# A third Strassen step per chunk couple, with the sums of raw weights on GpSimd

## The reference

```python
u = rms_norm(h, norm_mlp_g)
h = h + square(relu(u @ mlp_w1)) @ mlp_w2          # 2048 -> 8192 -> 2048
gate = sigmoid(rms_norm(h, ple_norm_g) @ ple_w_gate)
h = h + gate * (p @ ple_w_proj)
```

## Time and profile before

| | value |
|---|---|
| median of 3 runs | 1187.95 us |
| the profiled execution | 1187.82 us |
| its span, first to last instruction | 1186.1 us |
| PE busy | 1179.5 us, 5426 matmuls |
| DVE busy | 813.8 us |
| ACT busy | 631.5 us |
| POOL busy | 22.6 us, 31 instructions |
| granted TensorE clock | 1.000 |

### The profile page before, as it was taken

How to read it: one execution, slowest core, us unless ns; L and a number is a source line. 1 busy time by engine, 2 the same in 40 slices (tenths; PEclk the granted TensorE clock), 3 DMA queues, 4 the chain that set the end, 5 groups by cost and what they waited for, 6 DMA issues and landing times.

```text
span 1186.1 us, 14260 instructions
## 1 busy us (share of the span) xinstructions
PE 1179.5 (99%) x5426; PEld 979.4 (83%) x5426; DVE 813.8 (69%) x1123; ACT 631.5 (53%) x876; POOL 22.6 (2%) x31
## 2 busy tenths in 40 slices
PE   9999999999999999999999999999999999999998
PEld 7888888888888888888888888888888888888886
DVE  5568867888776567755688755679655788676554
ACT  6745455666655554643455633456533466455443
POOL 1000100000000000000000000000000000000000
PEclk9999999999999999999999999999999999999999
DMA  9867673334358666865477865477865476886661
GB/s 344 320 177 242 215 236 137 107 111 136 107 163 282 205 216 203 283 222 194 143 249 246 278 214 191 168 240 236 287 195 195 161 249 243 275 262 204 216 205 49
DMA packets 110980, 249.26 MB, mean 210 GB/s; under 512 B 9664, under 2 KB 55744, under 8 KB 110912
## 3 DMA queue, kind: packets, MB, share of 16 engines
q1 hardware_dynamic: 110768, 248.34, 63.4%
q10 hardware_dynamic: 144, 0.01, 0.0%
HBM read 233.63 MB, written 14.68 MB: 209 GB/s over the span
## 4 chain that ended last, share of the span: by engine, by line
PE 99%; DMA 0%; DVE 0%; SPq 0%; ACT 0%; issue 0%
PE acc L1777 59%; PE acc L1803 11%; PE sc L1777 7%; PE tr L1803 7%; PE sc L1803 7%; PE sc L2003 1%; PE sc L1968 1%; PE tr L1920 1%; PE tr L1909 0%; PE sc L1909 0%; PE tr L2055 0%; PE tr L2056 0%; DMA w_raw<-in_nsa_w_in_units_dram 0%; PE acc L1892 0%; PE tr L2032 0%; PE tr L2038 0%
## 5 line engine op out<-in xcount | busy, mean ns | idle before, releaser
L1167 DVE TENSOR_TENSOR w_split<-w_raw,w_split 128x1024 fp32r<-128x1024 f32 x296 | 358.8, 1220 | 211.0 <-ACT w_split L726 210.3
L726 ACT ACTIVATE w_split<-w_raw 128x1024 fp32r<-128x1024 f32 x296 | 309.8, 1057 | 255.7 <-PE acc L1777 195.4
L1777 PE MATMUL acc<-w_split,b_split 128*128 128x512 f32 x1536 | 355.3, 390 | 0.0
L1777 PEld LDWEIGHTS acc<-w_split,b_split 128*128 128x128 f32 x1536 | 287.2, 188 | 59.2
L1777 PE MATMUL acc<-w_split,a_hi 128*128 128x512 f32 x1020 | 318.2, 393 | 0.9 <-DVE w_split L1163 0.8
L1777 PEld LDWEIGHTS acc<-w_split,a_hi 128*128 128x128 f32 x1020 | 188.5, 188 | 40.4 <-issue 1.6
L1777 PE MATMUL acc<-w_split,a_lo 128*128 128x512 f32 x510 | 198.9, 390 | 0.0
L737 ACT ACTIVATE w_split<-w_raw 128x1024 fp32r<-128x1024 f32 x98 | 101.1, 1054 | 64.7 <-PE acc L1777 22.7
L1181 DVE TENSOR_TENSOR w_split<-w_raw,w_split 128x1024 fp32r<-128x1024 f32 x84 | 100.9, 1218 | 50.3 <-ACT w_split L737 50.3
L1777 PEld LDWEIGHTS acc<-w_split,a_lo 128*128 128x128 f32 x510 | 95.7, 188 | 20.4
L1803 PE MATMUL acc<-w_split,a_hi 128*128 128x512 f32 x316 | 97.3, 389 | 0.0
(11 more groups left out here) (253 smaller groups left out, 1061.6 us busy)
## 6 DMA issues: line engine op xcount, KB each, us to landing
w_raw<-in_mlp_w_units_dram SPq DMA_DIRECT2D x256, 512.0 KB, 4.4
w_raw<-in_nsa_w_in_units_dram SPq DMA_DIRECT2D x76, 512.0 KB, 4.7
w_raw<-in_nsa_w_out_units_dram SPq DMA_DIRECT2D x32, 512.0 KB, 4.4
w_raw<-in_ple_w_gate_units_dram SPq DMA_DIRECT2D x32, 512.0 KB, 4.2
turn_dram<-s SPq DMA_DIRECT2D x52, 128.0 KB, 3.4
turn_dram<-junk SPq DMA_DIRECT2D x44, 128.0 KB, 3.7
v_slc<-turn_dram SPq DMA_DIRECT2D x22, 256.0 KB, 3.8
v_win<-turn_dram SPq DMA_DIRECT2D x22, 256.0 KB, 4.6
```

What stands on the lines that cost most here:

```text
L726: nc.scalar.activation(w_hi[:, u % SPLIT], w_raw[:, u % RAW], ACT.Copy).then_inc(hi_done, 1)
L1167: nc.vector.tensor_tensor(w_lo[:, u % SPLIT], w_raw[:, u % RAW], f32(w_hi[:, u % SPLIT]), ALU.subtract).then_inc(lo_done, 1)
L1777: last = nc.tensor.matmul(banks_of(c)[t][:], xs[:, kt, toks], ws[:, u % SPLIT, m * NW:(m + 1) * NW], start=(kt == 0 and n == 0), stop=(kt ...
```

## The change

`QUADS` becomes (2, 4, 6): three of eight feature steps use Strassen's products, in all seven couples. The four sums of each step move from DVE's program to POOL's, in one loop over all 21 steps; POOL waits for `direct`, each sum waits for the one before, ACT waits for `sums` as it did. DVE goes on to `t_lo`, waiting for `sums_hi`. The hooks move by a unit or so, since a unit that opens a step has no hook. `a_full`, `r_raw` and `r_split` grow to three steps, and a few small tensors change places so that `t_split`, `r_split` and `mixed` still fit over the attention's tensors.

```diff
-QUADS = (4, 6)
+QUADS = (2, 4, 6)
...
+def quads(c):
+    return QUADS
...
-QUAD_UNITS = [FIRST[c] + 2 * k for c in PAIR_NO for k in QUADS]
+QUAD_UNITS = [FIRST[c] + 2 * k for c in PAIR_NO for k in quads(c)]
+QUADS_TO = {c: sum(len(quads(b)) for b in PAIR_NO if b <= c) for c in PAIR_NO}
...
 (sync, up_pair)
-                        hidden_turns(n, s, 12)
+                        hidden_turns(n, s, 13)
...
 (sync, down)
-                    if s == 0 and q:
+                    if s == 1 and q:
                         turn_back(n + 1)
...
 (gpsimd, between power(8) and power(9))
+            for at, u in enumerate(QUAD_UNITS):
+                b11, b21 = (w_raw[:, u % RAW, m * NW:(m + 1) * NW] for m in range(2))
+                b12, b22 = (w_raw[:, (u + 1) % RAW, m * NW:(m + 1) * NW] for m in range(2))
+                pool.wait_ge(direct, at + 1)
+                nc.gpsimd.tensor_tensor(b11, b11, b12, ALU.add).then_inc(first_sums, 1)
+                pool.wait_ge(first_sums, 2 * at + 1)
+                nc.gpsimd.tensor_tensor(b12, b12, b22, ALU.add).then_inc(first_sums, 1)
+                pool.wait_ge(first_sums, 2 * at + 2)
+                nc.gpsimd.tensor_tensor(b22, b11, b22, ALU.add).then_inc(sums, 1)
+                pool.wait_ge(sums, 2 * at + 1)
+                nc.gpsimd.tensor_tensor(b21, b22, b21, ALU.add).then_inc(sums, 1)
...
 (scalar, up_pair)
-                        if s in (3, 5):
-                            hidden_out(c - 2, s // 2 - 1)
-                        if s in (13, 14):
-                            turned_hidden(s - 13, q)
+                        if s in (3, 6):
+                            hidden_out(c - 2, s // 3 - 1)
+                        if s == 14:
+                            turned_hidden(0, q)
...
 (scalar, down_pair)
+                    if s == 0 and q:
+                        turned_hidden(1, q)
...
 (vector, split_lo_pair)
-                    b11, b21 = (w_raw[:, (u - 1) % RAW, m * NW:(m + 1) * NW] for m in range(2))
-                    b12, b22 = (w_raw[:, u % RAW, m * NW:(m + 1) * NW] for m in range(2))
-                    dve.wait_ge(direct, at + 1)
-                    nc.vector.tensor_tensor(b11, b11, b12, ALU.add).then_inc(first_sums, 1)
-                    dve.wait_ge(first_sums, 2 * at + 1)
-                    nc.vector.tensor_tensor(b12, b12, b22, ALU.add).then_inc(first_sums, 1)
-                    dve.wait_ge(first_sums, 2 * at + 2)
-                    nc.vector.tensor_tensor(b22, b11, b22, ALU.add).then_inc(sums, 1)
-                    dve.wait_ge(sums, 2 * at + 1)
-                    nc.vector.tensor_tensor(b21, b22, b21, ALU.add).then_inc(sums, 1)
                     for half, v in enumerate((u, u - 1)):
                         dve.wait_ge(sums_hi, 2 * at + half + 1)
                         nc.vector.tensor_tensor(t_lo[:, half], w_raw[:, v % RAW], f32(t_hi[:, half]),
                                                 ALU.subtract).then_inc(lo_done, 1)
                     yield s
...
 (vector, up_pair: mix(c) now stands behind the other hooks of s = 15)
-                        if s == 4:
+                        if s == 5:
                             turn_hidden(n + 1)
-                        if s == 14:
+                        if s == 15:
                             turned_hidden(1, 0)
...
-                        if s in (4, 6):
+                        if s in (5, 7):
                             turn_hidden(n + s // 2 - 2)
-                        if s == 14:
+                        if s == 15:
                             turned_hidden(0, q)
...
 (vector, down_pair)
-                    if s == 0 and q:
+                    if s == 1 and q:
                         turned_hidden(1, q)
...
 (tensor, up_pair)
-                    if k not in QUADS:
+                    if k not in quads(c):
                         for half in range(2):
                             plain_unit(FIRST[c] + 2 * k + half, k, half, banks)
                         continue
-                    if k == QUADS[0]:
+                    if k == quads(c)[0]:
```

More of the change, by code:

```diff
@@ L153 @@
 HALVED = 4
-REST = (4 * UW + 8 * N_QUADS * P + 4 * NW
-        - (4 * HPG * SEQ + 128 + 2 * NW + 2 * NW + 2 * SEQ + NW + TT * HPG * N_CMP + 2 * DK + SEQ))
+REST = 494
 X_ROWS = 7
@@ L234, in trunk_layer @@
         causal = sb("causal", [P, SEQ])
+        hid = sb("hid", [P, HID])
+        cmp_neg = sb("cmp_neg", [P, TT, N_CMP])
+        cmp_one = sb("cmp_one", [P, TT, N_CMP])
+        gates = sb("gates", [P, TT, GATES])
+        fold = sb("fold", [2 * HID + 1, HID])
         rest = sb("rest", [P, REST])
+        with nc.sbuf_tensor("p_raw", [P, 2, SEQ], F32) as p_raw, \
+                nc.sbuf_tensor("pt_hi", [P, 2, SEQ], F32R) as pt_hi, nc.sbuf_tensor("pt_lo", [P, 2, SEQ], F32R) as pt_lo:
+            pass
+        p_t = sb("p_t", [P, 2, NW + SEQ])
         v_slc = sb("v_slc", [P, TT, NW])
@@ L243, in trunk_layer @@
         s1 = sb("s1", [P, 2, 2, SEQ])
[L244 to L247, removed]
         kc_rows, kc_sq = junk_act[0:N_CMP], junk[0:N_CMP, 0:NW]
@@ L254, in trunk_layer @@
         cmp_c = sb("cmp_c", [P, TT * HPG])
-        gates = sb("gates", [P, TT, GATES])
         hid_e, hid_rows = s0[0:HID, 1, 0], s0[0:HID, 1, 1]
-        hid = sb("hid", [P, HID])
         hid_pair = p_t[:].rearrange("p b s -> p (b s)")[:, 2 * NW:].rearrange("p (g h c n) -> p g h c n", g=G, h=2, c=4)
         ident = sb("ident", [P, P])
-        cmp_neg = sb("cmp_neg", [P, TT, N_CMP])
-        cmp_one = sb("cmp_one", [P, TT, N_CMP])
-        fold = sb("fold", [2 * HID + 1, HID])
         const_t = sb("const_t", [P, N_CONST])
@@ L599, in up_pair @@
                             turn_back(n)
-                        if s == 12:
+                        if s == 13:
                             turn_away(n + 1)
-                        if s == 14:
+                        if s == 15:
                             turn_back(n + 1)
@@ L752, in keep_one @@
                 n, mixes = PAIR_NO[c], pair_banks(c)[1]
-                act.wait_ge(quad_used, N_QUADS * (n + 1))
+                act.wait_ge(quad_used, QUADS_TO[c])
                 nc.scalar.activation(mixed[:, 0], mixes[0][:], ACT.Copy).then_inc(one_copied, 1)
@@ L1068, in up_pair @@
                             hidden_alone(C_MLP + 1)
-                        if s == 13:
+                        if s == 15:
                             turned_hidden(1, 0)
                     if p and q:
-                        if s in (3, 5):
-                            hidden_out(c - 2, s // 2 - 1)
-                        if s in (13, 14):
-                            turned_hidden(s - 13, q)
+                        if s in (3, 6):
+                            hidden_out(c - 2, s // 3 - 1)
+                        if s == 14:
+                            turned_hidden(0, q)
             def down_pair(q):
@@ L1673, in up_pair @@
                 for s in split_lo_pair(c):
-                    if s == 2 * UPC - 1:
-                        mix(c)
                     if p and not q:
@@ L1690, in up_pair @@
                             pair_sums(c - 2)
-                        if s in (4, 6):
+                        if s in (5, 7):
                             turn_hidden(n + s // 2 - 2)
-                        if s == 14:
+                        if s == 15:
                             turned_hidden(0, q)
+                    if s == 2 * UPC - 1:
+                        mix(c)
             def down_pair(q):
@@ L1820, in quad @@
             def quad(c, i, banks, mixes):
-                n, k = PAIR_NO[c], QUADS[i]
-                u, at = FIRST[c] + 2 * k, N_QUADS * n + i
+                k = QUADS[i]
+                u = FIRST[c] + 2 * k
+                at = QUAD_UNITS.index(u)
                 def split(x, v, m):
@@ L1831, in quad @@
                 own, sums_of = (w_hi, w_lo), (t_hi, t_lo)
-                start, stop = i == 0, i == N_QUADS - 1
+                start, stop = k == quads(c)[0], k == quads(c)[-1]
                 c11, c21, c12, _ = banks
```

## The result

| | before | after |
|---|---|---|
| median | 1188.05 us (1187.4 to 1188.53, 4 runs) | 1240.28 us (1239.62 to 1240.7, 4 runs) |
| the profiled execution's span | 1186.1 us | 1238.9 us |

The changed kernel takes 1.0441 times the time of before (95% interval 1.0428 to 1.0453), 52 us more. The forecast was 1231 us, with a range of 1200 to 1258.

The account below looks back on a forecast made before the run. PE bounds the kernel, busy 1179.5 of 1186.1 us. From 1187.8 us, 4.8 us of matmuls go and 48.2 us of lateness (84T - 56.8 at T = 1.25) come: 1231 us, range 1200 to 1258.

Parts of the forecast that it names:

- What goes: On PE, one more Strassen step in each of seven couples removes 21 matmuls of 0.2267 us: 4.76 us.
- What waits: DVE and ACT run in order and stand until POOL's sums end; only PE's lead of at most four units overlaps.
- late parts: On PE, a step's last 12 matmuls, which need the sums; they had about 0.1 us to spare in the first step.
- T: On POOL, time from one dependent sum to the next: taken as 1.25 us, ends 0.73 and 1.85.
- D: End of DVE's half `w_lo` to end of second `t_lo`: 5.72 us before, forecast 4T + 2.52, 7.52 us.
- p = 0 couples: Couples without extra work between steps; the three with q > 0 were forecast late by 12T - 10.56 us each.
- p = 1 couples: Three couples with the previous couple's hooks around the new step: late by 12T - 5.27 us each.
- the clock rival: PE's clock falls after 6 us waits: 4 us more, 1235 us; upper price 27 us, 1258 us; chance 0.13.
- Edits at nothing: Grown tensors, the couple's closing `mix`, moved transposes and loads cost nothing; `mix` keeps some 0.2 us to spare.
- POOL at DVE's speed: Rival: POOL's sums take 0.69 us plus 0.2, losing 20.1 us, 1203 us; chance 0.10.
- the fixed price per instruction: Rival: each POOL TENSOR_TENSOR pays 0.39 us beside its elements; 66.7 to 98.6 us, 1250 to 1282 us; chance 0.17.
- not slower: Rival: PE's lead hides POOL's sums, needing sums of 0.21 us; 1183 to 1188 us; chance 0.05.

Follow-up runs that it names:

- e5: Kernel before with three steps in the three p = 0 couples, two elsewhere, sums on DVE, old hooks: 1185.93 us, ratio 0.9984.
- e6: Against e1, two hooks of the p = 1 couples moved one place later: 1194.65 us, ratio 1.0055 to the kernel before.
- e1: Changed kernel with the four sums back on DVE, third step and moved hooks kept: 1205.54 us, ratio 1.0147 to the kernel before.
- e4: Changed kernel with each POOL sum on 256 of its 512 columns, the rest left out: 1207.17 us, ratio 1.0164 to the kernel before.
- e2: Kernel before, two steps and its own hooks, with only the four sums moved to POOL: 1213.78 us, ratio 1.0218.
- e3: Changed kernel, ACT and DVE splitting the two units after a step before taking up its sums: 1283.55 us, ratio 1.0805 to the kernel before.

## Why the prediction was right

**What goes** (21 matmuls, 4.76 us) is right: 5426 matmuls became 5405, and e5 shows the price of nine.

**What waits** is right. By the view of waits ACT stood 124.3 us for POOL's sums and DVE 110.8 us for ACT's `t_hi`, in 21 waits each. PE's idle time before the late parts is 38.4 us in 16 waits, where 48 us were forecast. It is less than the lateness for two reasons: a wait delays the late part by some 0.3 us more than PE's idle time shows (an interval of 11.85 is 1.65 us over 10.2, with 1.35 us of idle time), and behind a slow stretch PE reached the late part late without standing idle, five times.

**The pitch** is the term that was mis-sized: T = 1.365 us against 1.25. The fixed part was right (0.19), the two inputs cost 2.57 passes, not two (1.10 instead of 0.85 us), and the hand-over on POOL took 0.08 us, not 0.2, which gave back half. With T = 1.365 the forecast's own sum is 84 x 1.365 - 56.8 = 57.9 us and 1240.9 us; measured 1240.3. That the two are so near is partly luck: an error in D covers two terms that the sum left out (below). The estimate worked out in the forecast from the Trainium skill (GPSIMD Engine Reference, "Performance versus the Vector engine"), 1237, was nearer than mine, and partly by luck too: a quarter of the time at four times the width leaves out the fixed part (1.12 us against 1.285), and 0.2 us for the hand-over was 0.12 too much.

**Lateness by kind of couple.** From late part to late part of the last steps, the span grew by 5.7 us over the first couple, 6.3, 4.6 and 4.3 over the p = 0 couples and 9.8, 10.6 and 11.2 over the p = 1 couples. The formulas give, with T = 1.365 and 0.68 us less for the three matmuls that a couple saves, 6.4, 5.1 and 10.4. So the hooks that fall between the steps were placed rightly, and they are e6's subject. (The first couple's line prices a pair of transposes at 1.23 us where the earlier trace rows show 1.30, and the clock rival's upper price has 11.7 us where its own formula gives 11.5; neither moves a result by more than 0.6 us.)

**Edits at nothing** failed once. I gave the couple's end 0.2 us to spare; the first couple overran it (ACT, DVE, PE):

```profile
481.50 0.60 ACT L773 ACTIVATE mixed<-acc 128x512 f32<-128x512 f32 x1 [2.48 <-PE acc L1814]
482.00 1.05 ACT L841 ACTIVATE b_split<-v_slc 128x1024 fp32r<-128x1024 f32 x1
...
483.08 1.23 DVE L1300 TENSOR_TENSOR b_split<-v_slc,b_split 128x1024 fp32r<-128x1024 f32 x1 [2.42 <-ACT b_split L841]
484.22 0.68 DVE L1238 TENSOR_TENSOR mixed<-acc,mixed 128x512 f32<-128x512 f32 x1
...
486.87 3.48 DVE L1188 TENSOR_TENSOR w_split<-w_raw,w_split 128x1024 fp32r<-128x1024 f32 x3
...
488.23 2.08 PE L1788 MATMUL acc<-w_split,b_split 128*128 128x512 f32 x8 [1.33 <-DVE w_split L1188]
```

DVE's `turned_hidden` (L1300) waited 2.42 us for ACT's own (L841), which stood behind `keep_one` (L773), and that waits for PE. In this couple the change moves ACT's hook from s = 13, ahead of `keep_one`, to s = 15, a line that the diff in "The change" leaves out; the forecast did not price it. `mix` then kept the next split until 488.1. That is 1.33 us, in this couple only, and it lies in the 6.3 of the next one. With the sums on DVE, the next late part comes 109.70 us on where the hook is moved (e1), and 108.13 with the hooks of the kernel before (e5).

**The rivals.** POOL at DVE's speed and the fixed price per instruction are out by e4. The clock was right as a mechanism and small: 0.05, 0.9 and 1.4 us in the three third steps (intervals of 11.89, 12.72 and 13.25 against 11.85), 2.3 us where 4 were worked out, mostly since in one of these couples the clock was back soon enough (12 matmuls in 4.38 us) for all of it to hide in the lateness that followed. The other three falls, behind waits of 1.8 to 2.5 us, which the forecast did not have, cost 0.1 us in all as far as the next intervals show. The Trainium skill's rule on an idle array (TensorE: Matmul & The Clock Gate, "The HAM clock gate") is that an array without work runs at the lower level, and these rows agree; which of two equal waits brings the clock down, no run here explains. The rival "not slower" needed sums of 0.21 us.

**What is left.** The forecast's lateness of 48.2 us, with 84 x 0.115 = 9.7 for the pitch, 1.3 for the first couple's end and 2.3 for the clock, makes 61.5. The span grew by 52.8 us with 4.8 us of matmuls taken off, 57.6. So these terms are 3.9 us too many in sum. Nearly all of that is D: the formula with T = 1.365 gives 7.98 us, and the 21 steps took 7.75 to 7.84, on average 7.81; 21 x 0.17 = 3.6 us. T already holds a hand-over behind each sum, and the formula adds one more, of 0.10, behind the fourth: ACT began 0.03 us after POOL's last sum (587.89 to 587.92).

## What to carry to other kernels

Work moved to an idle engine is off the path only if the engine that had it goes on to something else; where its next instruction waits for the result, the slower engine's time replaces the faster one's, whole. A step that just fits (0.1 us to spare) turns each added microsecond into lost time on the full engine, once per step. Before adding another such step, look at what hangs between the steps: with the sums on DVE (e1) it made three steps 4.3 us late each, 13 us, where the third steps win 4.8, and moving two hooks by one place gave back 11 us.

## What the runs showed of the hardware

- A two-input float32 addition on GpSimd took 0.19 us and 2.144 ns per element (738 ns for 256, 1287 for 512); VectorE's 128x512 took 0.69 us.
- GpSimd and VectorE delayed each other when both read two SBUF inputs: a split of 1.22 us took 2.11, a sum of 1.29 took 2.16. The Trainium skill (SBUF — State Buffer, "Who interferes with whom") describes such a lock; these rows agree.
- The length of a PE wait alone did not tell whether the granted clock fell behind it. Behind waits of 3.4 us, equal to 0.01 us, it was 0.62 over the next 12 matmuls in two cases and 1.00 in one (e1); behind waits of 1.84 us 0.65 to 0.68 in three cases and 1.00 in three (e2); behind waits of 2.70 us 0.61 to 0.65 in all seven second steps and 1.00 in all seven third steps (e3). Behind waits of 1.7 us it stayed at 1.00 (e6), and behind those over 3.6 us it was 0.50 to 0.63, save one of 3.62 us (e4) with 1.00.
